# Moving the large SBUF region by 192 bytes against the ring that feeds TensorE

## What is computed

```python
x = x + 0.5 * rmsnorm(swiglu(rmsnorm(x, g1), w1_gate, w1_up, w1_down), g1_post)
h = rmsnorm(x, g_mix_pre)
z = h @ w_in                      # pool channels | q | k | v
a = pool_mixer(z[pool]);  o = dilated_window_attention(q, k, v)   # 12 heads, 3 groups
x = x + rmsnorm(concat(a, o) @ w_out, g_mix_post)
x = x + 0.5 * rmsnorm(swiglu(rmsnorm(x, g2), w2_gate, w2_up, w2_down), g2_post)
```

## The kernel before, in words

| stage (lines) | weights | moving operand |
|---|---|---|
| gate and up, `product` (L1998 to L2000) | ring | xg, large region |
| its last columns, `tail_product` (L1956 to L1958) | tail_w, large region | xg, large region |
| down, `tile_product` (L2061 to L2063) | ring | ring |
| projection in, `weights_by_x` (L2091 to L2093) | ring | xe, large region |
| projection out (L2309 to L2311) | mhi and mlo, large region | ring |

## Time and profile before

### The profile page before, as it was taken

How to read it: one execution, slowest core, us unless ns; L and a number is a source line. 1 busy time by engine, 2 the same in 40 slices (tenths; PEclk the granted TensorE clock), 3 DMA queues, 4 the chain that set the end, 5 groups by cost and what they waited for, 6 DMA issues and landing times.

```text
span 1742.8 us, 21678 instructions
## 1 busy us (share of the span) xinstructions
PE 1705.2 (98%) x7949; PEld 1403.1 (81%) x7949; DVE 1117.9 (64%) x1409; ACT 711.9 (41%) x1256; POOL 625.0 (36%) x488
## 2 busy tenths in 40 slices
PE   8999999999999999999999899999999999999997
PEld 6888888888888888887888677788888888888886
DVE  7876665655568784424556667877656555657877
ACT  7433233332444553324434456533233333244453
POOL 3365554543352111118010201446545444345111
PEclk9999999999999999999999999999999999999999
DMA  6232233233853455332110265322343233484362
GB/s 214 69 110 91 91 120 128 91 101 108 317 181 97 149 149 162 121 99 73 50 60 14 61 204 182 106 88 91 100 133 107 91 115 103 140 301 141 101 230 91
DMA packets 160985, 216.98 MB, mean 125 GB/s; under 512 B 12848, under 2 KB 99056, under 8 KB 160880
## 3 DMA queue, kind: packets, MB, share of 16 engines
q1 hardware_dynamic: 153136, 188.73, 33.9%
q10 hardware_dynamic: 6896, 24.19, 3.9%
q0 software_dynamic: 848, 2.69, 0.5%
HBM read 162.09 MB, written 52.95 MB: 123 GB/s over the span
## 4 chain that ended last, share of the span: by engine, by line
PE 87%; DVE 6%; ACT 3%; issue 2%; POOL 1%; DMA 0%; ACTq 0%; SPq 0%; DVEq 0%; POOLq 0%
PE ps L1998 15%; PE ps L1999 14%; PE ps L2000 14%; PE ps L2061 7%; PE ps L2062 7%; PE ps L2063 7%; PE ps L2091 4%; PE ps L2093 4%; PE ps L2092 4%; PE ps L2201 2%; PE ps L2169 1%; PE ps L1956 1%; PE ps L1957 1%; PE ps L1958 1%; PE ps L2184 1%
## 5 line engine op out<-in xcount | busy, mean ns | idle before, releaser
L1998 PE MATMUL ps<-xg,ring 128*128 128x512 f32 x1120 | 440.7, 393 | 0.2
L1999 PE MATMUL ps<-xg,ring 128*128 128x512 f32 x1120 | 438.1, 391 | 0.0
L2000 PE MATMUL ps<-xg,ring 128*128 128x512 f32 x1120 | 436.8, 390 | 0.0
L2000 PEld LDWEIGHTS ps<-xg,ring 128*128 128x128 f32 x1120 | 210.2, 188 | 48.1
L1998 PEld LDWEIGHTS ps<-xg,ring 128*128 128x128 f32 x1120 | 210.4, 188 | 46.7 <-issue 1.4
L1999 PEld LDWEIGHTS ps<-xg,ring 128*128 128x128 f32 x1120 | 210.4, 188 | 44.1
L2061 PE MATMUL ps<-ring 128*128 128x512 f32 x616 | 240.4, 390 | 0.6 <-DVE ring L1167 0.6
L2062 PE MATMUL ps<-ring 128*128 128x512 f32 x616 | 239.7, 389 | 0.0
L2063 PE MATMUL ps<-ring 128*128 128x512 f32 x616 | 239.7, 389 | 0.0
L685 ACT ACTIVATE ring<-t_sum 128x512 fp32r<-128x512 f32 x160 | 100.3, 630 | 279.9 <-PE ps L2000 161.9
L1174 DVE TENSOR_TENSOR ring<-raw,ring 128x1024 fp32r<-128x1024 f32 x64 | 84.3, 1317 | 144.2 <-ACT ring L714 130.0
(11 more groups left out here) (218 smaller groups left out, 2782.2 us busy)
## 6 DMA issues: line engine op xcount, KB each, us to landing
st_op<-hd_dram SPq DMA_DIRECT2D x154, 256.0 KB, 2.7
raw<-in_w_gate_dram SPq DMA_DIRECT2D x20, 1024.0 KB, 6.5
raw<-in_w_up_dram SPq DMA_DIRECT2D x20, 1024.0 KB, 5.5
raw<-in_w_in_dram SPq DMA_DIRECT2D x40, 512.0 KB, 3.8
hd_dram<-u_b SPq DMA_DIRECT2D x64, 256.0 KB, 6.4
wd<-in_w_down_dram SPq DMA_DIRECT2D x18, 768.0 KB, 7.1
hd_dram<-hst SPq DMA_DIRECT2D x48, 256.0 KB, 6.4
raw<-in_w_out_dram SPq DMA_DIRECT2D x24, 512.0 KB, 3.7
```

The costliest lines, as they stand in the source:

```text
L1998: pe.matmul(acc, hi[:, a, :], x_hi, start=(a == 0 and not more), stop=False, skip_group_check=more)
L1999: pe.matmul(acc, hi[:, a, :], x_lo, start=False, stop=False, skip_group_check=more)
L2000: mm = pe.matmul(acc, lo[:, a, :], x_hi, start=False, stop=(a == HALF_D - 1), skip_group_check=more)
```

## The change

The region of the ring is made 48 float32 longer. Nothing lies in the added 192 bytes a partition. The large region, which comes behind it, begins 192 bytes later, and with it every tensor in it.

```diff
         q_even = over(16, "q_even", [P, 2, SEQ])
-        sb("region_ring", [P, 4 * D + 2 * (PAD + SEQ)])
+        sb("region_ring", [P, 4 * D + 2 * (PAD + SEQ) + 48])
```

## The result

The changed kernel takes 1735.09 us (median of 4 runs, 1733.60 to 1736.42), the kernel before in the same comparison 1746.13 (4 runs). The ratio is 0.994, 95% interval 0.9922 to 0.9957: 0.6% faster, 11.0 us, against 11.9 predicted.

A forecast was written before the change was run, and what follows sets the result against it. PE's matmul spacing was taken to bound the kernel; savings of 7.4 (gate and up), 2.0 (projection in) and 2.5 us (projection out), together 11.9, gave 1745.35 - 11.9 = 1733.4 us, said as 1733, with an 8-in-10 range of 1702 to 1765.

The forecast's parts named there:

- That only PE's spacing can move the end: Whole kernel: 87% of the span hangs on PE, so only how fast PE takes its instructions moves the end by much.
- That the distance of the regions is what sets the spacing: Gate and up, both projections: distance of weights from moving operand modulo 512 gives 226.7, 229 and 233.3 ns.
- The rival that something else sets it: Stages with crossing matmuls: distance is not the cause, 0 to 1.7 us saved, 1743.6 to 1745.4; chance that nothing moves 0.19.
- That 256 acts as 0: Crossing matmuls of gate and up and both projections: all take 226.7 ns at distance 256; chance 0.30 within 1 ns.
- The sum: Gate and up 7.4 us, projection in 2.0, projection out 2.5: together 11.9 us saved.
- a few tenths of the rest can be lost: Both projections: a few tenths of their saving can be lost where softmax sets the pace; gate and up's 7.4 us whole.
- Better than 0: Crossing matmuls: distance 256 beats 0, one step to 220.0 ns saves 43.4 us, about 1702; floor 1670; chance 0.24.
- Worse: Crossing matmuls: reads meet more at distance 256, all run at 233.3 ns, 19.1 us lost, 1764.5; chance 0.27.

The follow-up runs named there:

- the sign turned: Ring's region 384 bytes longer than in the kernel before, so weights lie 64 bytes ahead of the moving operand in gate and up: 1759.43 us.
- the run of 448 bytes: Ring's region 448 bytes longer than in the kernel before, so the distance is 0 modulo 512 in every stage: 1734.19 us, ratio 0.9939.
- the two other profiles with the old spacing: Against the kernel before: ring's region 256 bytes longer, 1742.66 us; and a 192-byte tensor put ahead of all tensors, 1742.98 us.
- those of 256 bytes: Ring's region 256 bytes longer than in the kernel before, so the regions lie 64 bytes apart modulo 256: 1742.66 us, one run.
- all moved: A 192-byte tensor put ahead of all tensors of the kernel before, every region moved and all distances kept: 1742.98 us, one run.
- 224, 160, 64 and 32 bytes more: Four runs with the ring's region longer by these lengths than in the kernel before: 1761.01, 1762.51, 1760.24 and 1759.90 us, in that order.

## Why the prediction was right

**That only PE's spacing can move the end.** Right. DVE's, ACT's and the transfers' times moved little (DVE's busy time from 1117.9 to 1121.5 us), and the stages with crossing matmuls moved.

**That the distance of the regions is what sets the spacing.** Argued from five rows before, shown since: with the sign turned the two values changed places, with all regions moved nothing happened. The rival that something else sets it had 0.19 and falls. One shape, one order and one count of instructions ran at 226.7, 228.9 and 233.3 ns for a change of some bytes in the place of the operands. That the reading of the weights and that of the moving operand meet in SBUF is the natural reading of this and is not shown; no run separates them. The Trainium skill says that the loading of the next weights takes nothing from the running matmul's reading (TensorE: Matmul & The Clock Gate, Part 2). What the prediction drew from this, that the distance could then matter nowhere, is not so in these runs; whether the two reads do take from each other stays open with the natural reading.

**That 256 acts as 0.** Right, and for the first of the two reasons: the pattern repeats every 256 bytes. The second, the scores whose keys lie 256 bytes apart, pointed the right way but could not have told 256 from any other value. Half of the scores of the last group of heads have their queries (q_even) in the ring's region and their keys in the large one, so their distance changed as the large region moved; their rows take 0.44 and 0.39 us in every profile. These float32 matmuls showed no dependence on the distance at all.

**The sum.** Gate and up -7.2 for -7.4, first half of the projection in -1.04 for -1.0; the run of 448 bytes repeats both (399.50 and 112.37 us). The second half and the projection out gave -0.4 for -3.5, and by the two other profiles with the old spacing nothing. The spacing in both fell as predicted. The step that was mis-sized is "a few tenths of the rest can be lost": it was 3.1 us in the profiled execution and may have been all 3.5. About 0.7 us of it go to the lower clock, by the estimate above. Waits take 1.7: 1.0 us more for mlo at L2309, 0.7 more for y at L1883. Some 0.7 us are not accounted for. From its 17th of 128 steps on, the projection out took 85.5 us in the changed kernel and in the run of 448 bytes, and 86.5 in those of 256 bytes and all moved: 1.0 us gained of the 2.1 that 6.2 ns for each of 336 matmuls would be. The steps ahead of that took 25.6 to 27.7 us, longer in the profiles of the new spacing, and took it back. The waits were on the table before the change: the prediction read L2061's 0.6 us and not L2309's 2.6, which stands in the earlier trace rows.

By the medians 0.9 us of 11.9 are missing, less than this comparison can tell. That they come so near is in part luck: 3.5 us of the sum belong to stages where the profiles show at most a small part of them, and 2.8 of the measured 11.0 lie in no stage that a profile shows. One slip changes nothing: the matmuls with weights in tail_w are 240 at L1956 to L1958 and 48 at L1942 to L1950, not 256.

**The rivals.** Better than 0: no tested distance is. Worse: at six of the eight distances tested modulo 256 the spacing is within about 1 ns of the 233.3 that it had. The prediction priced it at 19.1 us above before, at 1764.5; 224, 160, 64 and 32 bytes more gave 1759.9 to 1762.5. The chance of 0.27 was not idle: with 224 or 160 bytes in place of 192 the change would have been that rival.

## What to carry to other kernels

When matmuls of one shape follow each other at different distances in different stages, compare by start times, not by durations, and write beside each stage where weights and moving operand start. For fp32r operands streamed at 512 columns, put the two a multiple of 256 bytes apart and each at a multiple of at least 32 bytes; where tensors share regions of odd lengths, this is one pad. In a kernel that PE bounds, a spacing 1 to 3% shorter comes through whole in the stages where PE waits for nobody; where it waits for DVE, here in the attention and the projection out, the profiles show little or nothing of it.

## What was not expected of the hardware

The cost has no slope: 233.3 ns at 32 bytes on either side, 228.9 at -64 only. Starting both operands 16 bytes off costs down 4.4 ns a matmul and 4 bytes cost 11.1, at unchanged distance, while 32 bytes cost the last columns nothing. And a shorter weight load made the kernel slower by 11.1 us.
